# Refilling an expert's gate and up weights by two whole transfers, after both product halves, in a hybrid encoder layer with 32 experts

## What is computed

```python
D_MODEL = 1024; N_GROUPS = 4; EXPERTS_PER_GROUP = 8; TOP_K_FINE = 2; D_EXPERT = D_MODEL // 2

x = x + mix(rmsnorm(x, g1))                       # projection, three mixers, w_out
t = rmsnorm(x, g2)
# router: one group of 8 experts per token, in it the best two, with weights `gates`
for g in range(N_GROUPS):
    e = slice(g * EXPERTS_PER_GROUP, (g + 1) * EXPERTS_PER_GROUP)
    hg = jnp.einsum('td,edf->tef', t, w_gate[e])  # w_gate, w_up: (32, 1024, 512) f32
    hu = jnp.einsum('td,edf->tef', t, w_up[e])
    h = jax.nn.silu(hg) * hu * gates[:, g, :, None]
    y = y + jnp.einsum('tef,efd->td', h, w_down[e])   # w_down: (32, 512, 1024) f32
x = rmsnorm(x + y, final_norm_g)
```

## Time and profile before

| what | us |
| --- | --- |
| median of three runs (735.12 to 735.39) | 735.38 |
| span of the profiled execution, first to last instruction | 733.9 |
| the median run beyond that span | 1.5 |
| TensorE busy, share of the span | 81% |
| SP's part in the chain that ended last | 51% |

### The profile page before, as it was taken

How to read it: one execution, slowest core, us unless ns; L and a number is a source line. 1 busy time by engine, 2 the same in 40 slices (tenths; PEclk the granted TensorE clock), 3 DMA queues, 4 the chain that set the end, 5 groups by cost and what they waited for, 6 DMA issues and landing times.

```text
span 733.9 us, 8110 instructions
## 1 busy us (share of the span) xinstructions
PE 594.7 (81%) x3112; PEld 316.7 (43%) x3112; DVE 176.2 (24%) x322; ACT 107.1 (15%) x202; POOL 88.0 (12%) x146
## 2 busy tenths in 40 slices
PE   7999999999888999999776776778777777777820
PEld 5999999878753333333222222222222222222200
DVE  5554248514456010101000001000000100000037
ACT  6422342203210000000000000000000000000013
POOL 1000000000022212121121111111211111110000
PEclk9999999999979999999999999999999999999975
DMA  9930600286189999999999999999999999999756
GB/s 290 346 98 3 229 1 1 81 340 269 58 330 342 399 415 415 416 417 415 417 415 416 417 416 417 418 415 416 416 417 416 417 416 415 417 417 418 274 148 227
DMA packets 57128, 238.71 MB, mean 325 GB/s; under 512 B 9382, under 2 KB 16567, under 8 KB 40723
## 3 DMA queue, kind: packets, MB, share of 16 engines
q1 hardware_dynamic: 51987, 228.96, 78.9%
q0 software_dynamic: 5120, 9.46, 3.5%
HBM read 232.48 MB, written 13.24 MB: 335 GB/s over the span
## 4 chain that ended last, share of the span: by engine, by line
SPq 51%; PE 34%; DMA 6%; DVE 4%; issue 3%; ACT 1%; POOLq 0%; POOL 0%; DVEq 0%
SPq L458 33%; SPq L465 18%; PE ps L1283 12%; PE ps L1354 7%; PE ps L1445 5%; DMA w<-in_moe_w_up 3%; PE ps L1465 2%; PE ps L1380 1%; DMA y_rows<-ybuf,idc_y 1%; PE ps L1247 1%; PE ps L1249 1%; PE ps L1248 1%; DMA gain<-in_norm_g 1%; DVE yfin L826 1%; DVE x_sb L826 1%
## 5 line engine op out<-in xcount | busy, mean ns | idle before, releaser
L1445 PE MATMUL ps<-w,xT 128*64 128x512 f32 x1024 | 231.1, 596 | 57.5 <-DMA w<-in_moe_w_up 57.5
L1445 PEld LDWEIGHTS ps<-w,xT 128*64 128x64 f32 x1024 | 72.7, 137 | 214.1 <-issue 151.3
L1465 PE MATMUL ps<-wd,hexT 128*64 128x512 f32 x512 | 118.6, 604 | 27.7 <-DVE hexT L1164 27.7
L820 DVE TENSOR_TENSOR hexp<-silu_g,ps 128x256 f32<-128x256 f32 x32 | 13.5, 422 | 419.7 <-ACT silu_g L795 419.7
L594 POOL DMA_INDIRECT y_rows<-ybuf,idc_y x32 | 32.9, 1029 | 380.0 <-ACT ybuf L799 380.0
L1465 PEld LDWEIGHTS ps<-wd,hexT 128*64 128x64 f32 x512 | 38.1, 138 | 87.4 <-issue 52.8
L795 ACT ACTIVATE silu_g<-ps 128x256 f32<-128x256 f32 x32 | 12.3, 384 | 279.3 <-PE ps L1445 279.3
L1283 PE MATMUL ps<-hT_hi,wi_hi 128*128 128x288 f32 x224 | 48.7, 299 | 0.0
L1283 PE MATMUL ps<-hT_lo,wi_hi 128*128 128x288 f32 x224 | 48.0, 296 | 0.0
L799 ACT COPY ybuf<-ps 128x512 f32<-128x512 f32 x32 | 18.8, 586 | 179.6 <-PE ps L1465 179.6
L582 POOL DMA_INDIRECT xg<-hn_rows,idc_x x32 | 33.8, 1055 | 27.5 <-POOL idc_x L579 27.5
(11 more groups left out here) (194 smaller groups left out, 507.0 us busy)
## 6 DMA issues: line engine op xcount, KB each, us to landing
w<-in_moe_w_gate SPq DMA_DIRECT2D x64, 1024.0 KB, 18.9
w<-in_moe_w_up SPq DMA_DIRECT2D x64, 1024.0 KB, 23.7
wd<-in_moe_w_down SPq DMA_DIRECT2D x64, 1024.0 KB, 22.2
wo<-in_w_out SPq DMA_DIRECT2D x2, 2048.0 KB, 11.0
yfin<-y_rows SPq DMA_DIRECT2D x8, 512.0 KB, 6.0
x_sb<-in_x_prompt SPq DMA_DIRECT2D x4, 512.0 KB, 8.6
hn_rows<-hn2p SPq DMA_DIRECT2D x4, 512.0 KB, 3.0
out<-yfin SPq DMA_DIRECT2D x4, 512.0 KB, 2.6
```

The lines of the kernel that those rows point to most:

```text
L1445: last = mm(ps[64 * h:64 * h + 64, 1, :], lhs, w1[s][:, :, k, h * (F // 2):(h + 1) * (F // 2)], start=(k == 0), stop=(k == KD - 1))
L1465: last = mm(ps[64 * h:64 * h + 64, 3, :], lhs, wd[s][:, c, h * 512:(h + 1) * 512], start=(c == 0), stop=(c == F // P - 1))
```

## The change

For experts 3 to 31 (and for `block_past`, which doesn't run) `refill` no longer waits for `half_ps`. It waits for `gu_ps`, and then issues gate and up as one transfer of 2 MB each. `gate_up` waits for both semaphores ahead of its first product, and `half_ps` is gone. A whole transfer raises one semaphore by 16, where two half transfers raised it before, so the counts are 16 after a first fill of 32. The first fills of the three slots, the down weights and all other engines' work are as they were.

```diff
+            def load_whole(e, s):
+
+                for a in range(2):
+                    sp.dma_start(w1[s][:, a:a + 1, :, :].rearrange("p a k f -> p a (k f)"),
+                                 (gate_v, up_v)[a][:, bass.ds(e, 1), :]).then_inc(w1_in[s][a], 16)
+
             def refill(i, s):
-                sp.wait_ge(half_ps, NSLOT * (i - 1) + s + 1)
-                load_gate_up(NSLOT * i + s, s, halves=(0,))
                 sp.wait_ge(gu_ps, NSLOT * (i - 1) + s + 1)
-                load_gate_up(NSLOT * i + s, s, halves=(1,))
+                load_whole(NSLOT * i + s, s)
                 sp.wait_ge(dn_ps, NSLOT * (i - 1) + s + 1)
                 load_down(NSLOT * i + s, s)
...
             def gate_up(n, s, uses):
                 pe.wait_ge(xT_ready, n + 1)
+                for part in range(2):
+                    pe.wait_ge(w1_in[s][part], 16 * uses + 16)
                 for k in range(KD):
-                    if k % (KD // 2) == 0:
-                        pe.wait_ge(w1_in[s][k // (KD // 2)], 32 * uses)
                     lhs = xT[:, k % 4, 64 * (k // 4):64 * (k // 4) + 64]
                     for h in range(2):
                         last = mm(ps[64 * h:64 * h + 64, 1, :], lhs, w1[s][:, :, k, h * (F // 2):(h + 1) * (F // 2)],
                                   start=(k == 0), stop=(k == KD - 1))
-                    if k == KD // 2 - 1:
-                        last.then_inc(half_ps, 1)
                 last.then_inc(gu_ps, 1)
```

More of the change, by code:

```diff
@@ L335, in build @@
     order_ready = sem("order_ready")
-    half_ps, picks_ready, rows_step, rows_ready = (sem("half_ps"), sem("picks_ready"), sem("rows_step"),
+    picks_ready, rows_step, rows_ready = (sem("picks_ready"), sem("rows_step"),
                                                    sem("rows_ready"))
@@ L517, in block_past @@
                 e = sp.value_load(ovexp[0:1, bass.ds(b, 1)], min_val=0, max_val=NE - 1)
-                load_gate_up(e, 0)
+                load_whole(e, 0)
                 load_down(e, 0)
```

## The result

The changed kernel takes 737.63 us in the median of seven runs (736.52 to 738.67), the kernel before 735.38. The ratio is 1.0028, with a 95% interval from 1.0017 to 1.0039: 1.2 to 2.9 us slower, 2.1 in the middle. Twelve more runs, later and beside other variants (after_again), gave 1.0026 (1.0017 to 1.0035), 1.9 us. One execution of a later variant (first_again) took 1233.84 us and is not in that variant's ratio.

What follows compares the result with a forecast made beforehand. The prediction took a full stream of 29 weight refills, from about 229 us at 415 GB/s, as the bound, with TensorE following it. Its terms, 3.41 + 3.39 - 3.7 = +3.1 us on 735.4, gave 738.5 us, range 735.3 to 741.9.

Steps and rivals of the forecast that it cites:

- The first refill is asked for later: Start of the weight stream: first issue moves from 228.26 to 231.67, engines stand idle, all 29 refills move by +3.41 us.
- The later refills cost nothing: Middle of the stream: each later refill is asked for 3.65 us later, covered by a queue holding 21.8 us of work.
- The products begin when the whole is there: Last expert's gate and up: the whole 7.04 us come after the landing, where 3.65 were left before: +3.39 us.
- Fewer, longer packets: Weight stream on SP's queue: 522 packets fewer per engine, 7 ns each, -3.7 us; bounds nothing and 8.9 us.
- The fixed cost of a transfer: Weight transfers: the skill's about 2.0 us each, 58 fewer, 116 us less if paid one after the other; chance 0.01.
- TensorE's clock: Gate and up behind longer waits: a fall at the last expert, 740.2 (0.07); falls at every expert, 150 us more (0.01).
- The sign of being wrong that the prediction named: Middle experts: the clock falls for many of them and the interval between them grows over 16.1 us.
- 1: Weight stream: long rows gain nothing, only closing packets are saved, 0.4 us; +6.4, so 741.8 us; chance 0.14.
- 3: Gate and up stream loses all above its bytes, 8.9 us saved, which gives 733.3 us; chance 0.07.
- 5: Weight stream: 16 KB rows are slower; at 0.8 us a packet the stream would lose 80 us; chance 0.01.
- Rival 2: Weight stream: packets gain more, 5.3 us saved or more, the two losses about paid, 736.9 us or less; chance 0.17.

Runs made afterwards that it cites:

- after_again: The changed kernel itself, timed once more beside other variants on one chip: 737.38 us, ratio 1.0026 to the kernel before.
- first_again: The changed kernel with the first refill (expert 3) by halves, its first half asked for at `half_ps`, timed a second time: 735.65 us, ratio 1.0007.
- experiment 1: The kernel before with both half issues behind `gu_ps`, TensorE still waiting half by half, rows still 8 KB: 737.68 us, ratio 1.0034.
- experiment 5: The changed kernel with the first refill (expert 3) alone by halves: 735.35 us, ratio 1.0007; timed again, 735.65 us, ratio 1.0007.
- late_only: The run of experiment 1: the kernel before with both half issues behind `gu_ps`: 737.68 us, ratio 1.0034.
- rows8k: The changed kernel with its 2 MB transfers, each partition's 16 KB read from two places of 8 KB: 742.26 us, ratio 1.0103.
- experiment 2: The kernel before with TensorE waiting for both halves ahead of its first product, issues unchanged: 739.13 us, ratio 1.0051.
- experiments 6 and 8: The changed kernel with the last refill by halves (6), 734.18 us; with first and last by halves, 732.46 us, or first and last two, 731.74 us (8).
- experiment 3: The kernel before with both half issues behind `gu_ps` and TensorE waiting for both halves, rows still 8 KB: 741.13 us, ratio 1.0083.
- experiment 4: The run of rows8k: the changed kernel's whole transfers, each partition's 16 KB read as two runs of 8 KB: 742.26 us, ratio 1.0103.

## Why the prediction was right, and where its sizes were off

The forecast was 738.5 us, 3.1 more than before; measured were 1.9 to 2.3 more, on the side and within the range that it gave. The mechanisms are the ones it named; the sizes are not, and that the sum is only 1 us off is in part luck, as the steps show.

*The first refill is asked for later, +3.41.* The mechanism is there: the issue 3.4 us later and an empty stretch behind 228 us. The size is too large: alone it costs 2.5 us (experiment 1, interval 1.5 to 3.4), and in the changed kernel 1.5 (experiment 5). The step that failed is that all 29 refills "move by" the whole delay. It rests on the reading that the stream before is full from 229 us on, with one hole ahead. There is a second one from 237 to 243 us, mostly behind 239, where the earlier trace rows has no stretch: the kernel before moves 364 GB/s there and late_only 427. The late start doesn't have it, and by the rates that is 0.9 us of the 3.4.

*The later refills cost nothing.* Shown by experiment 1. In the changed kernel they land 30.9 us after their issue where it was 21.8, so more is outstanding, not less (rows8k has 28.0, so most of the growth comes with transfers twice as large):

```profile
L504 SPq DMA_DIRECT2D w<-in_moe_w_up x29: 337/1532/5642, 231.7 to 656.1; - x29
...
DMA to landing us min/median/max: 7.8/30.9/35.6
```

*The products begin when the whole is there, +3.39.* Alone 3.7 (experiment 2, interval 2.6 to 4.9), and half-wise waits at the end take it back (experiments 6 and 8). Without a fall of the clock the profiles have 3.3, as forecast; with one they have 5.0 to 5.1.

*Fewer, longer packets, -3.7.* The mechanism is shown by rows8k: long rows are the gain, fewer transfers none. The size is 4.0 by experiment 3, 5.5 by experiment 4 and 4.3 to 4.5 by the profiles, so this term was too small by about 0.7 us. With the profiles' 2.4 for the start and -4.4 for the rows the sum is +1.3 where the clock holds at the last expert and +3.0 where it falls; the measured 2.1 lies between. So two errors of 1.0 and 0.7 us in the same direction were partly paid back by a fall of the clock that the sum didn't have.

*The fixed cost of a transfer* plays no part here: rows8k has the fewer transfers and goes at 416 GB/s like the kernel before. The estimate of 116 us from the Trainium skill ("DMA: Bandwidth & Descriptors", section "Anatomy of one DMA") doesn't come about in this full queue.

*TensorE's clock* had 0.07 for a fall at the last expert. That was far too little: it is in four of seven profiles. The prediction took the one fall of the earlier trace rows as rare. In the changed kernel's profile the gate and up products took 8.4 us or more for 13 of the 24 experts from 324 us on, and the granted clock was 0.94 from 360 to 660 us. The 13 stand behind waits of 2.0 to 3.6 us; two others, behind waits of 3.1 us, kept their 7.09 (one is at 340.56 in the timeline above). That is nearer than I allowed to the rule of the Trainium skill ("TensorE: Matmul & The Clock Gate", section "HAM oscillation"): the trace agrees with it for about half of the experts. What a fall costs here is read from the rows, and that step held: it lengthens the products by 1.3 to 2.8 us, and the next wait is that much shorter. The sign of being wrong that the prediction named, a clock that falls for many experts and a longer interval between them, came in its first half only: the interval is (690.87 - 340.56) / 22 = 15.9 us against 16.1 before.

*The rivals.* 1, 3 and 5 are out: the rate did move, by 1.0% and upward, and long rows are not slower. Rival 2 was right that the rows save more than 3.7 us, but its 5.3 or more and its 736.9 or less did not come.

## What to carry to other kernels

In a stage that a full transfer queue bounds, a coarser refill costs nothing in the middle: its price is paid once where the queue starts empty and once behind the last landing. Look at these two places apart, and keep the fine pieces there (here for the first refill and the last two) and the long rows in between; that was 0.5% faster than the fine kernel and 0.8% faster than the coarse one. A wait that grows longer on TensorE should be checked at the last stretch for its clock, where no slack hides it.

## What the runs showed of the hardware that wasn't expected

- Rows of 16 KB move as one packet each on SP's queue. From 235 to 242 us of the changed kernel 185 of them and 16 tiny ones took 101.8% of 112 us, 616 ns each if the tiny ones are put at nothing, where two of 8 KB took 626:

```profile
DMA packets 202, 3.04 MB, mean 434 GB/s; under 512 B 16, under 2 KB 16, under 8 KB 16
## 3 DMA queue, kind: packets, MB, share of 16 engines
q1 hardware_dynamic: 201, 3.03, 101.8%
```

- How much SP may have outstanding isn't set by bytes alone. The down transfers are the same in all kernels, and the rates are within 1%; their median time from issue to landing is 22.2 us before, 24.2 in rows8k and 30.5 in the changed kernel:

```profile
wd<-in_moe_w_down SPq DMA_DIRECT2D x64, 1024.0 KB, 22.2
wd<-in_moe_w_down SPq DMA_DIRECT2D x64, 1024.0 KB, 24.2
wd<-in_moe_w_down SPq DMA_DIRECT2D x64, 1024.0 KB, 30.5
```

- A start of the stream that is later by 3.4 us ends it later by 1.5 to 2.5 us. The rates at 237 to 243 us account for the difference; no run tests why they differ.
